# The first layer's memory keys and values made in the experts' loop, behind its fourth pair, in plain fp32

## The reference

```python
def memory_cross_attention(q_mem, mem, w_kv):      # 4 heads of 64
    kv = mem @ w_kv                                # (256 x 1024) @ (1024 x 512)
    k, v = jnp.split(kv, 2, axis=-1)
    s = einsum('bshd,bmhd->bhsm', q, k) * HEAD_DIM ** -0.5
    return einsum('bhsm,bmhd->bshd', softmax(s), v)
```

## Time and profile before

| | us |
|---|---|
| median of 3 runs (lowest to highest) | 1879.21 (1878.42 to 1879.93) |
| the profiled execution, its own time | 1876.51 |
| its span, first to last instruction | 1874.7 |
| busy: PE / DVE / ACT | 1800.5 / 773.4 / 571.9 |
| moved by DMA | 592.40 MB, mean 316 GB/s |
| q8 and q14, instructions | 1.05 MB in 75 packets |

### The profile page before, as it was taken

The page is one execution under the profiler, slowest core; times in us unless marked ns, Lnnn a source line. Parts: engine busy times, 40 slices in busy tenths (PEclk is TensorE's granted clock), DMA queues, the critical chain, the costliest instruction groups (busy, mean ns, idle before and its releaser), DMA issues.

```text
span 1874.7 us, 24264 instructions
## 1 busy us (share of the span) xinstructions
PE 1800.5 (96%) x9774; PEld 1137.5 (61%) x9774; DVE 773.4 (41%) x1146; ACT 571.9 (31%) x913; POOL 16.5 (1%) x33
## 2 busy tenths in 40 slices
PE   7999999999999999989999999999999999999998
PEld 4799888733333333333333333327988888978886
DVE  3867655512112111121111111116676656676665
ACT  4444554410011110010100111105655545545552
POOL 0000001000000000000000000000000000000000
PEclk9999999999999999999999999999999999999999
DMA  9976755999999999999999999999356556336652
GB/s 351 332 253 231 240 198 190 348 426 427 431 431 430 431 430 431 430 430 429 430 431 430 431 430 430 431 429 338 129 179 201 181 201 202 125 103 206 197 170 100
DMA packets 155691, 592.40 MB, mean 316 GB/s; under 512 B 6735, under 2 KB 85775, under 8 KB 129120
## 3 DMA queue, kind: packets, MB, share of 16 engines
q1 hardware_dynamic: 153104, 582.90, 79.1%
q0 software_dynamic: 2512, 8.45, 1.5%
HBM read 590.26 MB, written 1.07 MB: 315 GB/s over the span
## 4 chain that ended last, share of the span: by engine, by line
PE 83%; DMA 9%; DVE 4%; ACT 1%; issue 1%; SPq 0%; DVEq 0%; ACTq 0%
PE psum L1810 20%; PE psum L1828 10%; PE psum L426 9%; DMA expert_ring<-in_w_mlp_dram 8%; PE psum L392 7%; PE psum L394 7%; PE psum L393 7%; PE psum L425 4%; PE psum L1792 3%; PE psum L410 2%; PE psum L412 2%; PE psum L411 2%; PE psum L1848 2%; DMA base<-in_w_ada_dram 1%; PE psum L1799 1%
## 5 line engine op out<-in xcount | busy, mean ns | idle before, releaser
L1810 PE MATMUL psum<-shared,expert_arena 128*64 128x512 f32 x1536 | 340.0, 595 | 8.3 <-DMA shared<-in_w_mlp_dram 8.3
L426 PE MATMUL psum<-layer_x_parts,layer_w_hi 128*128 128x512 f32 x704 | 240.5, 396 | 0.4 <-DVE layer_x_parts L2175 0.4
L1810 PEld LDWEIGHTS psum<-shared,expert_arena 128*64 128x64 f32 x1536 | 106.1, 137 | 220.3 <-issue 203.8
L1636 DVE TENSOR_SCALAR expert_arena<-psum 128x512 f32<-128x512 f32 x32 | 22.1, 692 | 524.8 <-PE psum L1810 524.8
L1531 ACT ACTIVATE expert_arena<-expert_arena 128x512 f32<-128x512 f32 x32 | 20.1, 629 | 498.4 <-DVE expert_arena L1636 498.4
L425 PE MATMUL psum<-layer_x_parts,layer_w_lo 128*128 128x256 f32 x616 | 171.8, 279 | 0.0
L353 DVE TENSOR_TENSOR mixer_w_lo<-mixer_ring,mixer_w_hi 128x1024 fp32r<-128x1024 f32 x96 | 116.3, 1223 | 87.7 <-ACT mixer_w_hi L348 87.3
L353 DVE TENSOR_TENSOR layer_w_lo<-slots_ahead,layer_w_hi 128x1024 fp32r<-128x1024 f32 x96 | 116.8, 1224 | 85.0 <-ACT layer_w_hi L348 85.0
L348 ACT CAST mixer_w_hi<-mixer_ring 128x1024 fp32r<-128x1024 f32 x96 | 99.9, 1048 | 152.1 <-PE psum L394 79.5
L426 PEld LDWEIGHTS psum<-layer_x_parts,layer_w_hi 128*128 128x128 f32 x704 | 125.8, 188 | 24.6 <-DVE layer_x_parts L2175 0.8
L392 PE MATMUL psum<-layer_w_hi,layer_x_parts 128*128 128x512 f32 (+1 forms) x368 | 134.2, 365 | 1.0 <-DVE layer_x_parts L2175 1.0
(11 more groups left out here) (324 smaller groups left out, 2629.2 us busy)
## 6 DMA issues: line engine op xcount, KB each, us to landing
shared<-in_w_mlp_dram SPq DMA_DIRECT2D x98, 2048.0 KB, 19.0
expert_ring<-in_w_mlp_dram SPq DMA_DIRECT2D x64, 2048.0 KB, 22.8
mixer_ring<-in_w_in_dram SPq DMA_DIRECT2D x38, 1024.0 KB, 5.9
slots_ahead<-in_w_mlp_dram SPq DMA_DIRECT2D x15, 2048.0 KB, 25.6
mixer_ring<-in_w_ada_dram SPq DMA_DIRECT2D x22, 1024.0 KB, 5.5
slots_ahead<-in_w_ffn_in_dram SPq DMA_DIRECT2D x22, 1024.0 KB, 4.9
memory_kv<-in_w_mlp_dram SPq DMA_DIRECT2D x15, 1024.0 KB, 24.7
kept<-in_w_mlp_dram SPq DMA_DIRECT2D x15, 1024.0 KB, 26.7
```

The costliest lines, as they stand in the source:

```text
L426: last = self.nc.tensor.matmul(out, hi, both[:, k].rearrange("p h s -> p (h s)"), start=k == 0, stop=k == KC - 1)
L1810: last = nc.tensor.matmul(U[CAP * h:CAP * h + CAP, N * n:N * n + N], xg[:, k, j, :], expert_slot(M, k // 2)[:, at:at + N], start=False, st ...
```

## The change

In the experts' loop SP loads the keys' and values' weights of layer 0 (1024x512, 2 MB) into `ahead` after expert 8's pieces, and expert 9's down pieces wait until PE has used them. Behind pair 3 PE transposes `mem` (16 blocks of 128x128, four to a bank), makes the keys transposed and the values (16 products each, 128 columns of weights, 256 moving, fp32), and waits until ACT has copied them out. The keys go to the last 512 columns of `shared`, the values to a new buffer `memory_values`, from where ACT copies them into `kv` behind the loop. `TURN` = 4 now parts the two orders on all engines: pairs 0 to 3 run in the first, 4 to 14 in the second. PE's branch stays behind pair 7. In layer 0 the jobs `km0` and `vm0` go, `un0` and `qm` come ahead of `wsT`, the scores ahead of `un1`; the norm of v moves to `un0t0`, `divide` to `un1t0` and `un1t1`. `memT` stays, since layer 1's keys and values need it.

```diff
@@ SP, one_round, first round
+                    loads_of(1, TURN)
+                    e = 2 * TURN
+                    for k in range(UP):
+                        up_load_freed(e, e, k, True)
+                    for k in range(DOWN):
+                        down_load(e, e, k, 0, True)
+                    sp.wait_ge(down_used, (e - 1) * DOWN + 1)
+                    sp.dma_start(M["ahead"][:, :], A["w_mem_kv_2"][0].rearrange("(p k) n -> p (k n)", k=KC)).then_inc(M["mem_here"], 16)
+                    for k in range(UP):
+                        up_load_freed(e + 1, e + 1, k, True)
+                    sp.wait_ge(memory_full, VALUES)
+                    for k in range(DOWN):
+                        down_load(e + 1, e + 1, k, 1, True)
+                    loads_of(TURN + 1, PAIRS - 1)
@@ ACT
+            def memory_rows_out():
+                for n in range(4):
+                    act.wait_ge(memory_full, n + 1)
+                    nc.scalar.copy(memT[:, 2 * n:2 * n + 2, :], bank[BG if n % 2 else BY].rearrange("p (k s) -> p k s", k=2)).then_inc(memory_out, 1)
+                act.wait_ge(memory_full, KEYS)
+                nc.scalar.copy(memory_keys(M), bank[BY].rearrange("p (a s) -> p a s", a=2)).then_inc(memory_out, 1)
+                act.wait_ge(memory_full, VALUES)
+                nc.scalar.copy(values_aside[:, :], bank[BG]).then_inc(memory_out, 1)
...
+            act.wait_ge(memory_out, VALUES)
+            act.wait_ge(down_used, (E - 1) * DOWN)
+            nc.scalar.copy(free(M["kv"], 512, T * W_MEM), values_aside[:, :])
@@ PE
+            def memory():
+                pe.wait_ge(M["mem_here"], 16)
+                pe.wait_ge(down_used, 2 * TURN * DOWN)
+                pe.wait_ge(xg_ready, 2 * TURN + 2)
+                for n in range(4):
+                    if n >= 2:
+                        pe.wait_ge(memory_out, n - 1)
+                    b = bank[BG if n % 2 else BY]
+                    for k in range(2):
+                        for t in range(T):
+                            at = 2 * n + k
+                            last = nc.tensor.transpose(b[:, N_MEM * k + P * t:N_MEM * k + P * t + P], mem_nat[:, t, at:at + KC * (P - 1) + 1:KC], ident)
+                    last.then_inc(memory_full, 1)
+                pe.wait_ge(M["mem_here"], 32)
+                pe.wait_ge(memory_out, 4)
+                for a in range(2):
+                    for k in range(KC):
+                        last = nc.tensor.matmul(bank[BY][:, N_MEM * a:N_MEM * a + N_MEM], w_mem[:, k, P * a:P * a + P], memT[:, k, :], start=k == 0, stop=k == KC - 1)
+                last.then_inc(memory_full, 1)
+                for t in range(T):
+                    for k in range(KC):
+                        last = nc.tensor.matmul(bank[BG][:, W_MEM * t:W_MEM * t + W_MEM], memT[:, k, P * t:P * t + P], w_mem[:, k, W_MEM:2 * W_MEM], start=k == 0, stop=k == KC - 1)
+                last.then_inc(memory_full, 1)
+                pe.wait_ge(memory_out, VALUES)
...
-            pairs_of(0, 0, MIDDLE)
+            pairs_of(0, 0, TURN)
+            memory()
+            later_pairs_of(0, TURN, MIDDLE)
@@ layer 0, the order of the jobs
-        jobs.add("km0", "act", jobs.wide(w_kv[0], 0))
+        jobs.pair("un0", "act", jobs.rows(w_in, 0))
+        jobs.add("qm", "act", jobs.wide(w_in, 2 * W_MIX))
         for n in range(3):
             jobs.add(f"wsT{n}", "dve")
         jobs.add("bsT", "dve")
-        jobs.pair("un0", "act", jobs.rows(w_in, 0))
-        jobs.add("qm", "act", jobs.wide(w_in, 2 * W_MIX))
-        jobs.pair("un1", "act", jobs.rows(w_in, N, W_MIX - N))
         scores(0)
         scores(1)
+        jobs.pair("un1", "act", jobs.rows(w_in, N, W_MIX - N))
         for n in range(3):
             jobs.add(f"sv{n}", "dve")
-        jobs.pair("vm0", "act", jobs.rows(w_kv[0], W_MEM, W_MEM))
         weights_over(0)
@@ DVE and ACT, the norm of v (and, on ACT, its roots)
-                if name == "km0":
+                if name == "un0t0":
@@ DVE, divide
+                if name[:4] == "un1t":
+                    divide(int(name[4]))
...
-                    if n != 1:
-                        divide(n // 2)
```

More of the change, by code:

```diff
@@ L1306, in experts @@
     own = ctx.enter_context(nc.sbuf_tensor("expert_own", [P, 2, P], F32R))
+    values_aside = ctx.enter_context(nc.sbuf_tensor("memory_values", [P, T * W_MEM], FP32))
+    mem_nat, memT = free(M["base"], 0, T, D), free(M["kept"], 0, KC, N_MEM)
+    w_mem = free(M["ahead"], 0, KC, 2 * W_MEM)
     b1, b2 = bias[:, 0:D], bias[:, D:D + N]
@@ L1466, in one_round, with loads_of @@
                     up_load_freed(i0 + 1, 1, k, True)
-                with sp.Fori(1, PAIRS - 1) as q:
-                    for odd in range(2):
-                        e = sp.snap(q * 2 + odd)
-                        for k in range(UP):
-                            up_load_freed(i0 + e, e, k, True)
-                        for k in range(DOWN):
-                            down_load(i0 + e, e, k, odd, True)
+                def loads_of(begin, end):
+                    with sp.Fori(begin, end) as q:
+                        for odd in range(2):
+                            e = sp.snap(q * 2 + odd)
+                            for k in range(UP):
+                                up_load_freed(i0 + e, e, k, True)
+                            for k in range(DOWN):
+                                down_load(i0 + e, e, k, odd, True)
+                if later:
+                    loads_of(1, PAIRS - 1)
+                else:
+                    loads_of(1, TURN)
[6 more added lines that the diff above has]
+                    sp.dma_start(M["ahead"][:, :], A["w_mem_kv_2"][0].rearrange("(p k) n -> p (k n)", k=KC)).then_inc(M["mem_here"], 16)
+                    for k in range(UP):
+                        up_load_freed(e + 1, e + 1, k, True)
+                    sp.wait_ge(memory_full, VALUES)
+                    for k in range(DOWN):
+                        down_load(e + 1, e + 1, k, 1, True)
+                    loads_of(TURN + 1, PAIRS - 1)
                 for e in range(E - 2, E):
@@ L1544, in one_round @@
                     flag.append(second_flag(act))
-                with act.Fori(0, MIDDLE) as p:
+                with act.Fori(0, TURN) as p:
                     i = i0 + p * 2 + 1
@@ L1552, in one_round @@
                     aT_out(i + 1)
-                with act.Fori(MIDDLE, PAIRS - 1) as p:
-                    i = i0 + p * 2 + 1
-                    gather_out(r * PAIRS + p + 1, 0)
-                    sigmoid(i)
-                    aT_out(i)
-                    gather_out(r * PAIRS + p + 1, 1)
-                    sigmoid(i + 1)
-                    aT_out(i + 1)
+                if isinstance(r, int):
+                    memory_rows_out()
+                with act.Fori(TURN, PAIRS - 1) as p:
+                    turned(p)
                 i = i0 + E - 1
@@ L1651, in one_round, with turned @@
                 i0 = r * E
+                def turned(p):
+                    e = p * 2 + 1
+                    i = i0 + e
+                    gatedT_out(i - 1, 0)
+                    gate(r, e)
+                    dve.wait_ge(gathered, (r * PAIRS + p + 1) * 2)
+                    choose(r, p + 1)
+                    dve.wait_ge(down_used, (i - 1) * DOWN + 1)
+                    choose_own(e + 1, 0)
+                    y_out(i - 1)
+                    activate(i)
+                    gatedT_out(i, 1)
+                    gate(r, e + 1)
+                    dve.wait_ge(down_used, i * DOWN + 1)
+                    choose_own(e + 2, 1)
+                    y_out(i)
+                    activate(i + 1)
                 if not isinstance(r, int):
@@ L1668, in one_round @@
                     flag.append(second_flag(dve))
-                with dve.Fori(0, MIDDLE) as p:
+                with dve.Fori(0, TURN) as p:
                     e = p * 2 + 1
```

40 lines of the change are left out of this document (19 added, 21 removed).

## The result

The changed kernel takes 1889.42 us (median of 5 runs, 1888.22 to 1891.52) against 1879.21 (5 runs): 10.2 us more. Compared in pairs the ratio is 1.0062, 95% interval 1.0051 to 1.0073. Forecast were 1884.4 and a range from 1878.5 to 1891.0: the sign is right, the size is half of what came. The profiled execution took 1890.07 us, its span is 1888.3 us, against 1876.51 and 1874.7 before. In the spans the difference is 13.6 us, since the profiled execution of before lay 2.7 us under its median, and that of after 0.65 over.

A forecast was written before the change was run, and what follows sets the result against it. Bound by the DMA in the experts' loop and by PE in layer 0. The loop's +9.3 us (7.6 plus a 1.7 half-clock stretch) less the layer's 4.1 gave +5.2, so 1884.4 us, range 1878.5 to 1891.

The forecast's parts named there:

- The signs named in advance: Right: 4.9 us more DMA, dip near 634, loop's end 7 to 11 later, layer idle some 7; wrong: gap over 3.
- Bound by the DMA in the loop, by PE in layer 0: Experts' loop runs at the DMA's 430 GB/s; in layer 0 PE is busy throughout from 1282.64 to 1370 us.
- The load, 4.88 us: Experts' loop: 2.10 MB more at 430 GB/s adds 4.88 us, hidden by nothing as the DMA is never idle.
- The new load comes about 0.8 us late: DMA queue near 600 us: the load waits for expert 7's down buffer and starts about 0.8 us late.
- PE's block, 17.8 us: New block behind pair 3: transposes 3.2, products 13.8, last copy and handovers 0.8, from 604.3 to 622.1 us.
- The gap behind it: DMA gap of 1.5 us before expert 10's first up piece near 634 us, plus 0.4 at the following pieces.
- The branch takes 6.9: PE's branch in the loop: 4.67 us idle, then a group taking 9.33 instead of 7.09, as in the kernel before.
- a second fetch: Rival: new code at pair 4 stalls PE as the branch does, 6.9 us reach the end; +12, 1891; chance 0.12.
- 1.6 us to spare: Loop's end: PE's lag about 19 plus 6.9 at the branch, less 10 and 17.5 regained, leaves 1.6 us.
- One more half-clock stretch: Second order in the loop, now eleven pairs: one more stretch at 1.2 GHz, 1.7 us; none and three as bounds.
- Layer 0, +4.1: Layer 0: 11.5 us of products go, new waits of 7.4 come, gain 4.1; bounds 11.5 and 1.
- The sum: Whole kernel: loop +9.3 less layer 4.1 gives +5.2 us, median 1884.4; the forecast keeps 0.54.

The follow-up runs named there:

- after_shifted: The changed kernel with 32 never-executed instructions added in the untaken side of PE's branch, which moves its target: 1885.17 us, 1.0034 of the kernel before.
- first_order: after_shifted with pairs 4 to 7 put back into the first order on PE, ACT and DVE: 1884.51 us, 1.0040 of the kernel before.
- before_shifted_2: The kernel before with 184 never-executed instructions in the untaken side of PE's branch, target at place 186: 1881.81 us, 1.0025 of the kernel before.
- piece_first: after_shifted with the first 2 MB piece of expert 9 issued ahead of the memory's weights: 1889.11 us, 1.0059 of the kernel before.

## Why the prediction was half right

- **The signs named in advance.** DMA time of 4.9 us, a dip near 634 us, and waits in the layer (5.75 us against some 7), 3.31 of them released by ACT, came. The loop's end came 17.2 us later, not 7 to 11. Just behind the block the queue was dry for 2.7 to 3.2 us, around the 3 us that were to count as wrong, while PE itself had no such gap.
- **Bound by the DMA in the loop, by PE in layer 0: right.** The load alone costs 0.41%, and PE's usual stall at the branch costs nothing in the kernel before (0.9995 without it).
- **The load, 4.88 us: right.** Its bytes and the dry time add up to the loop's end within 0.1 us in after_shifted.
- **"The new load comes about 0.8 us late": wrong, 3.2.** I compared the time at which the last queued piece lands (599.85) with the time at which the load's first bytes move. A piece counts as landed well after its last bytes have begun to move: the queue is dry from 597, 2.8 us ahead of that. SP issued the load 0.9 us later than the row of before, and 2.4 us pass from the issue to the bytes. The latency had to stand on one side of the comparison only. (The landing itself, 609.4 less two pieces of 4.88, is 599.6.) What makes the delay matter is that SP stands at this wait with nothing else issued behind 573.
- **PE's block, 17.8 us: 18.4.** The gap behind it, forecast at 1.5 + 0.4, was 2.7 to 3.2, at the place named, for the reason named: `first_order` takes it away by freeing the slot about 8 us earlier.
- **"The branch takes 6.9": wrong, and the largest miss.** It took 11.25 us idle and 1.3 at half clock (8.36 for 7.09). I had a second fetch among the rivals, but at the new block, where no idle time of that kind came, and had taken the branch's own cost as fixed because its code does not change. Its place does. By my own bookkeeping PE had 1.6 us to spare, so 4.0 of the added 5.6 had to come out at the end. Moving the target gave back 5 in the medians, together with what the next point tells. The half clock is not the branch's alone: without a branch the same product takes 8.78, behind waits of 0.93 and 0.61.
- **One more half-clock stretch: three more came.** The clock is at half for 3.4 us at 916.4, 974.4, 1032.5, 1090.5 and 1148.5, once in each of five pairs, where before it was two in seven. In after_shifted none of these is there. The same place in both kernels, kernel after first:

```profile
916.33 0.75 PE L1874 MATMUL psum<-expert_bias,expert_own 128*128 128x512 f32 x1 [0.86 <-DVE expert_arena L1679]
917.01 8.47 PE L1880 MATMUL psum<-expert_ring,expert_arena 128*64 128x512 f32 x32
...
912.57 0.47 PE L1874 MATMUL psum<-expert_bias,expert_own 128*128 128x512 f32 x1 [0.61 <-DVE expert_arena L1679]
912.98 7.09 PE L1880 MATMUL psum<-expert_ring,expert_arena 128*64 128x512 f32 x32
```

  So the second order alone does not bring them. At 1.7 us each the three more are 5.1 us of PE's time, nearly as much as the 5.6 of the branch, and the 5.4 us of dry time at the branch and ahead of the loop's end are the price of both; no run parts them. What brings the stretches is open. The second fetch goes with them, since before_shifted_2 has three at once (905.4, 963.5, 1021.5). But `piece_first` has two (915.8, 973.8) without it, and PE being late does not suffice, since in after_shifted too it waits for no transfer until 1185.5. The Trainium skill (TensorE: Matmul & The Clock Gate, A second HAM failure mode) tells of short idle times between groups of matmuls that make the clock go down and up. That fits the stretches in kind; that it would be worse in the second order as such is not borne out.
- **Layer 0, +4.1: 3.6.** The waits were 3.31, 0.26 + 1.38, 0.40 and 0.40, forecast as 3.6, 1.1, 1.5, 0.6, 0.6, so 5.75 against 7.4 in sum. The scores behind the first wait then ran at half clock, 3.60 instead of 2.1, which I had only among the bounds. Smaller waits (+1.65) and this (-1.5) would leave the gain at 4.2; the missing 0.6 is not accounted for. The reason given for the waits is shown: in the old order they shrink to one of 2.48.
- **The sum.** Forecast +9.3 - 4.1 = +5.2. In the profiles it is +17.2 - 3.6 = +13.6: the dry times at the load and behind the block were 3.7 larger, the branch and what follows it 5.4 against 1.7, and 0.5 is left over. In the medians it is +10.2, so the size was half of what came. That the result lies in the range is luck: its upper end was set by a second fetch at the new block, and by three more half-clock stretches with a poor layer. A second fetch came, at the branch, and three more stretches came, but with 3.6 us from the layer.
- **Slips without effect.** The range's lower end by its own terms is 1879.3 (7.6 - 7.5 above the median), not 1878.5, and the chances within 0.2% add up to 0.35 (0.26 + 0.05 + 0.04), not 0.33.

## What to carry to other kernels

Where a loop runs at the DMA's pace, ask of every moved block not how long TensorE takes for it but which buffer comes free later than its place in the queue. Here that was 3 us of dry queue at the load, where SP stood with four issuable pieces behind it, and 3 behind the block. A buffer freed earlier removed such a stretch, while sending one piece first only moved it and made it larger (8.7 us against 6.0). An order of jobs need not be changed because work is taken out of it: here the old one, with two products less, gave a layer of 85.8 to 87.0 us, the new one 90.6 to 93.4. And before a change is judged by half a per cent, move the branch targets: instructions that are never executed were worth 0.3% here. With all of this put right the change as a whole is level with the kernel before (0.9993, 0.9984 to 1.0002).

## What the runs showed of the hardware

- The idle time at PE's one branch out of the loop is 4.6 to 5.8 us where PE goes on behind the first q8 packet of 16 KB, and 9.8 and 11.25 us where it goes on behind the second. Four instructions decided between them (places 190 and 186), and two different kernels agree at the same place. The Trainium skill (Runtime: NRT & Kernel Launch, Instruction fetch mechanics) says that instructions come in blocks of 16 KiB, 256 of them, and that a taken branch outside the window forces a fetch. The trace's packets agree; that a second may be needed, and what one costs while the DMA is saturated, is what these runs add.
- A turn of a pair on PE has 516 recorded instructions (258 matmuls and as many weight loads), more than two blocks of 256. (From 1290 us on, where the code runs straight, 27 q8 packets go with 7136 recorded instructions of PE, 264 for each.) The turns show no such gap, and no q8 packet starts between 422 and 840 us in the kernel before. The prediction read the same section by its window of two blocks; the section also gives TensorE room for 2048 instructions, and that is what the turns agree with.
- A wait of 3.3 us on PE in layer 0 was followed by products at 1.2 GHz in all six kernels with the new order (3.58 to 3.92 us for 2.10); a wait of 2.48 in the same layer was followed by such a stretch in one of three kernels.
